# Two-layer hybrid trunk (attention, RWKV-7, DeltaNet, experts): passes, masks and odd projection reordered

## The chip, the cores and the metric

The kernel runs on one core of a Trainium2 chip. The metric is device microseconds for one execution. The kernel before takes 1800.96 us (median of 3 runs, 1800.35 to 1801.52). The engines are TensorE (PE), VectorE (DVE), ScalarE (ACT), GpSimd (POOL) and SyncE (SP, which issues the DMAs here).

## The reference, cut to what matters

Input x is 256 tokens of 1024 numbers, float32. Two layers follow each other.

- Even layer: h = rmsnorm(x); one projection gives q, k, v of 8 attention heads of 64 and r, k, v of 8 RWKV heads of 64. The attention output and the output of a bidirectional RWKV-7 scan are concatenated, projected and added to x. Then a dense SwiGLU of width 2816 is added.
- Odd layer: h = rmsnorm(x); one projection (1024 to 3600) gives, in chunks of 512 columns, c_b, c_c, c_x (a short gated convolution: y_c = c_b * conv3(c_c * c_x)), q, k, v of 4 DeltaNet heads of 128, a gate z, and 16 columns of beta and alpha. q, k, v go through conv3 and SiLU, q and k are scaled to unit length, and a chunked gated delta rule runs in both directions. Both parts are projected and added to x. Then the top 2 of 8 SwiGLU experts of width 3584 are added.

```
state = state * w + (state @ a) b^T + v k^T          # RWKV-7 step; y = state @ r
lhs = tril(kb k^T * decay, -1) + I                    # DeltaNet, per chunk
u = lhs^-1 (v * beta - (kb * exp(gc)) @ state)
o = (q * exp(gc)) @ state + (q k^T * decay) @ u
state = state * exp(glast) + (k * exp(glast - gc))^T u
```

Both scans are computed with chunks of 128 tokens. Every chunk of every head then needs the inverse of a unit triangular 128x128 matrix. There are 2 directions x 2 chunks x 8 heads of them for RWKV and 2 x 2 x 4 for DeltaNet.

## The kernel before, in words

The five engines run one program each, tied by semaphores. What an engine does next is the order in which its program is written; nothing is planned by a tool.

**Inverses.** The 16x16 blocks on the diagonals of all the matrices of a mixer are inverted together on DVE (`block_inverses`, L1312 to L1345: gather the blocks with a transpose, three doublings by products and sums, two transposes). Then three doubling levels (16 to 32, 32 to 64, 64 to 128; `lev` 4, 5, 6) run on PE, two groups `g` of four heads at a time. In a level POOL masks the matrix (`level_masks`, L630 to L642), PE multiplies it with the inverse so far (`X`, L2015), ACT copies X from PSUM, PE multiplies again (`PT`, L2027 and L2030), and DVE adds the result to P and T (`inv_adds`, L1360 to L1371). `expand` (L1347 to L1358) writes the block inverses as block-diagonal 128x128 tiles P and T.

**RWKV passes.** Four passes p = 0..3, one per (direction, chunk): (0,0), (1,1), (0,1), (1,0). Pass p needs, in order: the three levels of its inverse; the rest R (PE L2089, L2093) and its copy on ACT (L852); the update U = inverse x R (L2101) and its copy (L856); for p < 2 the states (L2110, L2112); the outputs (L2117, L2122, L2124), which DVE adds into `yab`. The score matrices are masked by DVE (`mask_scores`, L1373 to L1378), three masks m = 0, 1, 2 per pass: m = 0 is for the rest, 1 and 2 for the outputs. In the kernel before PE does all of a pass's levels, then waits for all six masks (two groups, three m) and then does rest, updates, states and outputs, group by group. After passes 0 and 1 it computes the scores of pass p + 2 (`score`, L2053, L2057), after pass 0 also `tokens(1)` (L2064), after pass 2 the transposes of the attention half (L2136). The attention output is scaled by 1/den (`attended`, L1303 to L1310) inside `block_inverses`, ahead of its second doubling. The output projection (`ev_half`, L2154) follows pass 3.

**Odd mixer.** PE: beta and alpha (L2242), then `od_in(0)` to `od_in(5)` (L2252; chunks in the order c_b, c_c, c_x, q, k, v; each is four column blocks of 128 in eight products of 256 columns, copied out by ACT, L917, from four PSUM banks in turn), with the sums of the gates after chunk 1 (L2268, L2270) and the squared lengths of q and k (`lengths`, L2260, a product with all ones into 128 partitions) between chunks; then z (L2282), k k^T and k q^T (L2290, L2291), transposes of k and v (L2298), the decay rows (L2306) and the beta rows (L2314). DVE does the short convolution (L1515 to L1525), then the convolutions of q, k, v as they come (`shift_mix`, L1140 to L1145), squares, reciprocals of 1024 columns (L1542), scales, then the decay differences (L1565, L1567), the matrices to invert `Ao` (L1577 to L1583), the gather (L1590), the block inverses, and the two inversion passes p = 4, 5 (`invert`), which PE starts at L2015 again. The recurrence, the gated norm, the output projection (L2359) and the router follow, and then 8 experts of about 124 us each, which load their weights in 336 DMAs of 1024 KB.

**Memory.** `arena`, `scr`, `ring`, `ehf` and `xn` are reused from stage to stage; `Tb` (the blocks to invert) lies in `Am`, the tile into which POOL writes its masked matrices; `attn` lies in the tile of hT, the input of all projections.

Of the kernel before, what the change touches and what calls it, by code (L numbers as in the profile page):

```python
# [8 lines left out]
ACT = mybir.ActivationFunctionType  # L9
# [33 lines left out]
NHOME = 4  # L43

# [10 lines left out]
    ("red_rdy qk_sum qk_rdy mix_rdy kinv_rdy mixv_rdy bon_rdy bon_cp ya_rdy blk_rdy ln1_sum y1_rdy ln0_sum yab_rdy "  # L55
     "sp_y g_rdy gc_rdy yc_rdy qk2_rdy blk2_rdy on_sum yd_rdy rt_max as_rdy").split())}
# [21 lines left out]
def static_chunks():  # L78
# [9 lines left out]
    if UPTO >= 3:  # L88
        out += [("od_in", n, 1) for n in range(7)] + [("od_out", n, 1) for n in range(2)]
# [3 lines left out]
def hybrid_trunk(nc, A, out):  # L93
# [19 lines left out]
    with ctx:  # L113
# [60 lines left out]
        class Region:  # L174
# [5 lines left out]
            def take(self, *shape):  # L180
# [4 lines left out]
                if len(shape) > 1:  # L185
# [79 lines left out]
        qkvr, qkvc, cbx = g_o.take(12, SEQ), g_o.take(12, SEQ), g_o.take(12, SEQ)  # L265
        cu, zt = g_o.take(4, SEQ), g_o.take(TT, 512)
        g_o2 = Region(arena, 0, 3072)
        Ao = g_o2.take(2, 8, P)
        Do = [g_o2.take(4, P) for _ in range(2)]
        Ug = Do  # L270
        attn = [[hT_f[:, 512 * (2 * i + g):512 * (2 * i + g) + 512].rearrange("p (u s) -> p u s", u=4)
                 for g in range(2)] for i in range(2)]
# [6 lines left out]
        kqm = [g_o4.take(4, P) for _ in range(TT)]  # L279
        Ro = [g_o4.take(4, P) for _ in range(2)]  # L280
# [6 lines left out]
        glog, nbeta = sm.take(TT, 8), sm.take(TT, 8)  # L287

# [30 lines left out]
        dve_const = sem("dve_const")  # L319
# [43 lines left out]
        ex_rdy = sem("ex_rdy")  # L363
# [35 lines left out]
        conv_rdy, silu_rdy, l2_sq, l2_ps, l2_std = (sem(n) for n in (  # L399
            "conv_rdy", "silu_rdy", "l2_sq", "l2_ps", "l2_std"))  # L400
# [32 lines left out]
        SC_BANK = [(0, 1, 2, 4), (4, 5, 6, 7)]  # L433
# [8 lines left out]
        def used_up(kind, n):  # L442
# [4 lines left out]
                    "od_in": (cv_ps, 2 * n + 2) if n < 6 else (z_ps, 2), "od_out": (o_ps, 8 + 2 * n + 2)}[kind]  # L447
# [130 lines left out]
        def _(pool):  # L578
# [19 lines left out]
            for a in range(TT):  # L598
# [10 lines left out]
                               pattern=[[-1, P]], channel_multiplier=1)  # L609
            link(pool.memset(bones[:, :], 0.0))  # L610
# [19 lines left out]
            def level_masks(p, mats, blocks):  # L630

                Am = INVB[p][3]
                for lev in range(LEV0, NLEV):
                    for g in range(2):
                        if lev > LEV0:
                            pool.wait_ge(x_ps, inv_seq(p, lev - 1, g))
                        elif p % 4 == 0:
# [6 lines left out]
            pool.wait_ge(dve_const, 1)  # L644
# [15 lines left out]
        def _(act):  # L660
# [167 lines left out]
            def score_copies(q):  # L828
                for i in range(8):
# [3 lines left out]
                    act.activation(scb[q % 2][i // 4][:, i % 4], B[SC_BANK[q // 2][i % 4]][:, 0:3 * P].rearrange(  # L833
# [67 lines left out]
            if UPTO >= 3:  # L901
# [3 lines left out]
                ba = B[6][:, 0:TT * 16].rearrange("p (a n) -> p a n", a=TT)  # L905
# [7 lines left out]
                def od_copies(m0, m1):  # L913
                    for m in range(m0, m1):
                        act.wait_ge(cv_ps, m + 1)
                        dst = cbx[:, 2 * m:2 * m + 2, :] if m < 6 else qkvr[:, 2 * m - 12:2 * m - 10, :]
                        act.activation(dst, B[m % 4][:, :].rearrange("p (t s) -> p t s", t=2),  # L917
                                       ACT.Copy).then_inc(cv_sb, 1)
# [6 lines left out]
                def od_length(i):  # L925
                    for n in range(2):
                        act.wait_ge(l2_ps, 2 * i + n + 1)
                        act.activation(xn[:, i, 512 * n:512 * n + 512], B[(6, 0)[i] + n][:, :], ACT.Sqrt,
                                       bias=eps_col[:, 0:1]).then_inc(l2_std, 1)

                od_copies(0, 5)
                act.wait_ge(dve_step, DVE_STEPS["gc_rdy"])
                act.activation(ge, gt, ACT.Exp).then_inc(act_step, 1)
                od_copies(5, 8)
                od_silu(0)
                od_copies(8, 10)
                od_length(0)
                od_silu(1)
                od_copies(10, 12)
# [128 lines left out]
        def _(dve):  # L1068
# [231 lines left out]
            for h in range(4, HA):  # L1300
                head_scores(h)
# [1237 lines left out]
```

## Time and profile before

| what | value |
|---|---|
| runs | 1800.35 to 1801.52 us, median 1800.96 |
| profiled execution | 1797.01 us, of which the span is 1795.3 us |
| mean granted TensorE clock | 0.963 of full |
| PE busy | 1704.0 us (95%) |
| DVE busy | 1306.4 us (73%) |
| ACT busy | 967.0 us (54%) |
| POOL busy | 78.9 us (4%) |
| DMA | 428.78 MB, mean 239 GB/s |

PE is busy almost everywhere. In the 40 slices of the span (44.9 us each) its busy tenths are below 7 in one place only, the fifteenth and sixteenth slice (628 to 718 us, digits 5 and 6). The granted clock is in tenths of full speed: 1.00 is 2.4 GHz and 0.50 is 1.2 GHz. The even mixer runs to 332 us, the dense SwiGLU to 527 us, the odd mixer and router to 788 us, and the experts to the end.

### The profile page before, as it was taken

What the parts mean: (1) busy time and instruction counts of PE and PEld (TensorE: products, weight loads), DVE (VectorE), ACT (ScalarE), POOL (GpSimd) and SP (SyncE); (2) the same over time, 40 slices, a digit from 0 to 9 for tenths busy, and PEclk for the clock granted to TensorE, in tenths of its full rate; (3) what the DMA queues carried; (4) which work ended last, traced back from release to release, by engine and by line L of the source; (5) the groups of instructions that cost most, each with busy time, mean ns of one, the idle gap of its engine ahead of it and who ended that gap; (6) DMA issues with size and microseconds to landing.
All of it is one profiled execution on the core that took longest, in us unless ns stands there. A gap on an engine that the chain in (4) does not pass through costs nothing.

```text
span 1795.3 us, 22588 instructions
## 1 busy us (share of the span) xinstructions
PE 1704.0 (95%) x8728; PEld 1414.3 (79%) x8728; DVE 1306.4 (73%) x1232; ACT 967.0 (54%) x905; POOL 78.9 (4%) x92
## 2 busy tenths in 40 slices
PE   7998999999999956989999999999999999999997
PEld 3867988699988835668888888888888888888886
DVE  5587555544430677468898888898888988888985
ACT  2455221444331231157767677777677677677773
POOL 1013321000000003000000000000000000000000
PEclk9998888999999988989999999999999999999999
DMA  6410002455542310089999999999999999999992
GB/s 230 136 59 0 1 1 94 140 184 185 190 169 94 141 47 1 7 287 372 369 334 367 376 330 362 352 353 366 336 363 375 322 369 375 326 368 353 346 372 100
DMA packets 199502, 428.78 MB, mean 239 GB/s; under 512 B 10746, under 2 KB 34574, under 8 KB 199438
## 3 DMA queue, kind: packets, MB, share of 16 engines
q1 hardware_dynamic: 199438, 427.90, 66.3%
q8 instruction: 44, 0.72, 0.2%
q14 instruction: 20, 0.16, 0.0%
HBM read 426.82 MB, written 1.05 MB: 238 GB/s over the span
## 4 chain that ended last, share of the span: by engine, by line
PE 91%; DVE 6%; ACT 1%; issue 1%; POOL 0%; DMA 0%; SPq 0%; DVEq 0%; ACTq 0%
PE bank L2416 17%; PE bank L2418 17%; PE bank L2417 17%; PE bank L2252 5%; PE bank L2185 4%; PE bank L2186 3%; PE bank L2184 3%; PE bank L2425 2%; PE bank L1842 2%; PE bank L2015 2%; PE bank L1833 2%; PE bank L2359 2%; PE bank L2154 2%; PE bank L2461 1%; PE bank L2030 1%; PE bank L2027 1%
## 5 line engine op out<-in xcount | busy, mean ns | idle before, releaser
L1778 DVE TENSOR_TENSOR split<-ring,split 128x2048 fp32r<-128x2048 f32 x336 | 763.8, 2289 | 113.3 <-ACT split L1051 109.7
L1051 ACT ACTIVATE split<-ring 128x2048 fp32r<-128x2048 f32 x336 | 640.2, 1924 | 175.5 <-PE bank L2418 173.9
L2416 PE MATMUL bank<-split 128*128 128x512 f32 x896 | 354.4, 395 | 2.7 <-DVE split L1752 1.4
L2418 PE MATMUL bank<-split 128*128 128x512 f32 x896 | 349.6, 390 | 0.0
L2417 PE MATMUL bank<-split 128*128 128x512 f32 x896 | 348.9, 389 | 0.0
L2416 PEld LDWEIGHTS bank<-split 128*128 128x128 f32 x896 | 168.3, 188 | 36.4 <-issue 1.7
L2418 PEld LDWEIGHTS bank<-split 128*128 128x128 f32 x896 | 168.2, 188 | 35.9
L2417 PEld LDWEIGHTS bank<-split 128*128 128x128 f32 x896 | 168.5, 188 | 33.5
L2416 PE MATMUL bank<-split,ehr_ 128*128 128x512 f32 x448 | 180.3, 402 | 0.0
L2418 PE MATMUL bank<-split,ehr_ 128*128 128x512 f32 x448 | 174.9, 391 | 0.0
L2417 PE MATMUL bank<-split,ehr_ 128*128 128x512 f32 x448 | 174.6, 390 | 0.0
L1469 DVE TENSOR_TENSOR ringr<-ring,split 128x2048 fp32r<-128x2048 f32 x33 | 75.5, 2293 | 90.0 <-ACT split L882 89.8
L2185 PE MATMUL bank<-ringr,split 128*128 128x256 f32 (+1 forms) x440 | 135.1, 307 | 0.0
L882 ACT ACTIVATE split<-ring 128x2048 fp32r<-128x2048 f32 x33 | 63.1, 1921 | 84.2 <-DMA ring<-in_ev_ffn_up 44.0
L2416 PEld LDWEIGHTS bank<-split,ehr_ 128*128 128x128 f32 x448 | 84.0, 188 | 28.1 <-DVE split L1778 10.5
L2184 PE MATMUL bank<-ehr_,split 128*128 128x256 f32 x352 | 99.1, 282 | 1.4 <-DVE ringr L1087 1.4
L2186 PE MATMUL bank<-ehr_,ringr 128*128 128x256 f32 x352 | 99.4, 282 | 0.0
L2418 PEld LDWEIGHTS bank<-split,ehr_ 128*128 128x128 f32 x448 | 84.1, 188 | 18.5
L2417 PEld LDWEIGHTS bank<-split,ehr_ 128*128 128x128 f32 x448 | 84.2, 188 | 15.9
L2185 PEld LDWEIGHTS bank<-ringr,split 128*128 128x128 f32 x440 | 83.6, 190 | 3.8
L2252 PE MATMUL bank<-scr,ring 128*128 128x256 f32 x384 | 85.5, 385 | 0.0
L2252 PEld LDWEIGHTS bank<-scr,ring 128*128 128x128 f32 x384 | 74.2, 194 | 10.8 <-issue 0.5
(461 smaller groups left out, 2153.3 us busy)
## 6 DMA issues: line engine op xcount, KB each, us to landing
ring<-in_od_moe_gate SPq DMA_DIRECT2D x112, 1024.0 KB, 7.0
ring<-in_od_moe_up SPq DMA_DIRECT2D x112, 1024.0 KB, 7.3
ring<-in_od_moe_down SPq DMA_DIRECT2D x112, 1024.0 KB, 6.6
ring<-in_od_w_in SPq DMA_DIRECT2D x7, 2048.0 KB, 7.8
ring<-in_ev_w_in SPq DMA_DIRECT2D x6, 2048.0 KB, 9.0
ring<-in_ev_ffn_gate SPq DMA_DIRECT2D x11, 1024.0 KB, 5.4
ring<-in_ev_ffn_up SPq DMA_DIRECT2D x11, 1024.0 KB, 7.9
ring<-in_ev_ffn_down SPq DMA_DIRECT2D x5, 2048.0 KB, 7.9
```

The lines of the kernel that those rows point to most:

```text
L882: act.activation(homes[q % NHOME], ring[:, v], ACT.Copy).then_inc(pc_hi, 1)
L1051: act.activation(wst[:, r % NSTAGE, 0, :], ring[:, (r % NHALF) * HALF:(r % NHALF + 1) * HALF], ACT.Copy).then_inc(w_hi, 1)
L1469: dve.tensor_tensor(ringr[:, v], ring[:, v], homes[q % NHOME].bitcast(F32), SUB).then_inc(pc_lo, 1)
L1778: dve.tensor_tensor(wst[:, r % NSTAGE, 1, :], ring[:, (r % NHALF) * HALF:(r % NHALF + 1) * HALF], wst[:, r % NSTAGE, 0, :].bitcast(F32), S ...
L1833: last = pe.matmul(B[banks[a]][:, :], hT[:, k, P * a:P * a + P], w8[:, k, :], start=(k == 0), stop=(k == KT - 1))
L2184: pe.matmul(o, sh, mh, start=start, stop=False, skip_group_check=True)
L2185: pe.matmul(o, sh, ml, start=False, stop=False, skip_group_check=True)
L2186: return pe.matmul(o, sl, mh, start=False, stop=stop, skip_group_check=True)
L2252: last = pe.matmul(B[m % 4][:, SEQ * (f % 2):SEQ * (f % 2) + SEQ], w8[:, k, P * f:P * f + P], hT[:, k, :], start=(k == 0), stop=(k == KT - 1))
L2416: pe.matmul(o, hi, wh, start=start, stop=False)
L2417: pe.matmul(o, hi, wl, start=False, stop=False)
L2418: return pe.matmul(o, lo, wh, start=False, stop=stop)
```

## The change

The maths is the same. In the RWKV part:

- PE's program for a pass is cut into pieces (`level_x`, `level_pt`, `rests`, `updates`, `outputs_v`, `outputs_u`, `states_v`, `states_u`) and put in another order. The rests stand inside level 6, between X and PT. The products with v stand before those with U. Each piece waits only for its own mask and group.
- DVE does one mask kind after each level. The tiles P and T of the next pass are expanded as soon as the one of them that the pass doesn't use, or no longer uses, is free. Two blocks of terms for the layer norm move from pass 2 into passes 0 and 1.
- `attended` moves behind the block inverses; it is one half per group. The clearing of `Tb` moves into the attention heads. `Tb` moves to `xn`, and POOL's first masks no longer wait for the block inverses.
- The scores of passes 1 and 3 use other banks or the same banks in another order, with other waits.

In the odd mixer:

- The projection order is q, k, c_c, c_x, c_b, v, z (`OD`), in pairs of column blocks and two banks. ACT writes the middle term of the convolutions while copying, and does the squares. The lengths of q and k are 8 rows instead of 128 equal ones: one reciprocal of 8x256, which PE then broadcasts.
- Decay rows, lengths, k k^T, k q^T, beta rows and the transposes of k stand between the projection chunks on PE. ACT gathers the blocks with 16 copies, so that DVE transposes them in one instruction. The block inverses and the short convolution stand ahead of v on DVE.
- `attn`, `Do`, `cbx`, `zt` move to other memory.

The diff, cut to its core ("..." marks what is left out):

```diff
+OD = (3, 4, 1, 2, 0, 5)
...
-        out += [("od_in", n, 1) for n in range(7)] + ...
+        out += [("od_in", n, 1) for n in OD + (6,)] + ...
...
+                        elif p == 0:
+                            pool.wait_ge(vt_sb, 2)
+                            pool.wait_ge(q_rdy, 4)
+                            pool.wait_ge(dve_step, DVE_STEPS["bon_cp"])
+                        elif p == 4:
                             pool.wait_ge(dve_step, DVE_STEPS[blocks])
...
+                def tile_copies(t):
+                    act.wait_ge(cv_ps, t + 1)
+                    n = OD[t // 2]
+                    src = B[t % 2][:, :].rearrange("p (t s) -> p t s", t=2)
+                    if n < 3:
+                        m = 4 * n + 2 * (t % 2)
+                        last = act.activation(cbx[:, m:m + 2, :], src, ACT.Copy)
+                    else:
+                        m = 4 * (n - 3) + 2 * (t % 2)
+                        act.activation(qkvr[:, m:m + 2, :], src, ACT.Copy)
+                        for i in range(2):
+                            b = cd + 12 + m + i
+                            last = act.activation(qkvc[:, m + i, :], src[:, i, :], ACT.Copy, scale=cols[:, b:b + 1])
+                    last.then_inc(cv_sb, 1)
...
+                for i in range(4):
+                    act.wait_ge(ao_rdy, i + 1)
+                    for k in range(4):
+                        r = slice(32 * k, 32 * k + 32)
+                        last = act.activation(strided(Qc2[r], 4 * i, (16, 2), (32, 32), (1, 4)),
+                                              strided(Ao[r], 512 * i + 32 * k, (0, 2), (1, 32), (P, 4)), ACT.Copy)
+                    last.then_inc(qc_rdy, 1)
+                tile_copies(7)
...
+            block_inverses(gather_all, None, whole(Xm), Tb, whole(Tm), Xs, Tc, Pc).then_inc(dve_step, 1)
+            dve.wait_ge(dve_step, DVE_STEPS["blk_rdy"])
+            for g in range(2):
+                expand_p(0, g, Pc)
+            for g in range(2):
+                expand_t(0, g, Tc)
+                attended(g)
+            for p, (z, c) in enumerate(RW):
+                inv_adds(p, 4)
+                mask_scores(p, 0)
+                inv_adds(p, 5)
+                mask_scores(p, 1)
+                inv_adds(p, 6)
+                mask_scores(p, 2)
...
+            for p, (z, c) in enumerate(RW):              # PE
+                for lev in range(LEV0, NLEV):
+                    for g in range(2):
...
+                        level_x(p, lev, g)
+                    if lev == NLEV - 1:
...
+                        for g in range(2):
+                            rests(p, g)
+                    for g in range(2):
+                        if lev == LEV0 and p == 0:
+                            if g == 0:
+                                pe.wait_ge(sc_sb, 15)
+                            else:
+                                pe.wait_ge(dve_step, DVE_STEPS["ya0_rdy"])
+                        level_pt(p, lev, g)
                 if p < 2:
+                    outputs_v(p, 0)
+                    outputs_v(p, 1)
+                    updates(p, 0)
+                    updates(p, 1)
                     pe.wait_ge(tok_sb, 2 * p + 2)
+                    states_v(p, 0)
+                    states_v(p, 1)
+                    states_u(p, 0)
+                    states_u(p, 1)
                 else:
+                    outputs_v(p, 0)
+                    updates(p, 0)
+                    updates(p, 1)
+                    outputs_v(p, 1)
+                outputs_u(p, 0)
+                outputs_u(p, 1)
...
+                od_pair(0)                                # PE, odd projection
+                od_pair(1)
...   (sums of the gates)
+                od_pair(2)
+                od_pair(3)
...   (decay rows)
+                od_pair(4)
+                for i in range(2):
+                    pe.wait_ge(l2_sq, i + 1)
+                    for h in range(HD):
+                        j = HD * i + h
+                        last = pe.matmul(B[2][0:HA, 0:SEQ], oneh[:, 7 - j:15 - j], xn[:, i, SEQ * h:SEQ * h + SEQ],
+                                         start=(j == 0), stop=(j == 2 * HD - 1))
+                last.then_inc(l2_ps, 1)
+                od_pair(5)
+                pe.wait_ge(dve_step, DVE_STEPS["linv_rdy"])
...   (8 products of 256 columns that broadcast the reciprocal lengths)
+                od_pair(6)
...   (k k^T, k q^T, beta rows)
+                od_pair(7)
+                pe.wait_ge(kk2_sb, 2)
+                for i in range(2):
+                    turn_tokens(i, 4)
+                for t in range(8, 12):
+                    od_pair(t)
+                pe.wait_ge(ao_rdy, 4)
...   (z; transposes of v; then the passes p = 4, 5)
```

## Rows read from the trace of the kernel before

**Rows 1.** RWKV stages: stretch, length, PE, PEld, DVE, ACT, POOL busy, clock, DMA.
```profile
174.10:192.65 18.55, 16.84 (x129) 16.43 (x129) 14.45 (x18) 3.16 (x6) 11.23 (x7) 0.87 0.00 1
192.65:210.59 17.94, 17.79 (x121) 16.99 (x121) 6.35 (x12) 5.01 (x12) 0.00 (x0) 0.74 0.01 1
210.59:243.78 33.19, 30.57 (x242) 29.58 (x240) 16.03 (x26) 8.39 (x19) 8.84 (x6) 0.90 0.01 1
243.78:279.40 35.62, 33.76 (x218) 33.26 (x217) 17.89 (x29) 6.27 (x14) 8.88 (x6) 0.73 0.01 2
279.40:303.71 24.31, 24.31 (x209) 24.08 (x209) 16.66 (x29) 5.91 (x12) 6.46 (x4) 0.98 0.24 86
```

**Rows 2.** TensorE's timeline, RWKV passes: start, duration, engine, line, count, [idle].
```profile
174.10 3.95 PE L2015 MATMUL bank<-arena 128*128 128x128 f32 x16 [4.83 <-POOL arena L642]
...
192.65 3.64 PE L2093 MATMUL bank<-scr,arena 128*128 128x64 f32 x16 [1.71 <-issue]
...
206.07 1.04 PE L2064 MATMUL bank<-ident,ring 128*128 128x128 f32 x8
207.05 0.70 PE L2053 MATMUL bank<-ring 64*128 64x256 f32 x4
...
210.59 2.05 PE L2015 MATMUL bank<-arena 128*128 128x128 f32 x16
...
216.12 2.17 PE L2015 MATMUL bank<-arena 128*128 128x128 f32 x16
...
227.40 1.97 PE L2093 MATMUL bank<-scr 128*128 128x64 f32 x16 [1.80 <-DVE scr L1378]
...
260.60 0.77 PE L2089 MATMUL bank<-scr,ring 128*128 128x128 f32 x2 [1.86 <-DVE arena L1378]
...
277.70 1.91 PE L2136 MATMUL bank<-ident,scr 128*128 128x128 f32 x8
```

**Rows 3.** VectorE's timeline, 159 to 211 us.
```profile
159.44 0.25 DVE L1305 RECIPROCAL small<-small 128x16 f32<-128x16 f32 x1 [1.04 <-PE bank L1936]
...
170.84 0.99 DVE L1345 STREAM_TRANSPOSE scr<-arena 128x512 f32<-128x512 f32 x1
171.87 6.73 DVE L1355 TENSOR_TENSOR arena<-scr,bmask 128x512 f32<-128x512 f32 x4
...
187.91 4.63 DVE L1378 TENSOR_TENSOR arena<-arena,smask 128x512 f32<-128x512 f32 x4
...
206.62 3.90 DVE L1355 TENSOR_TENSOR arena<-scr,bmask 128x512 f32<-128x512 f32 x4
```

**Rows 4.** Busy time by stage of the odd mixer.
```profile
539.56:655.30 115.74, 114.35 (x533) 93.88 (x532) 47.55 (x87) 32.54 (x47) 0.00 (x0) 0.98 0.31 109
655.30:685.68 30.38, 0.02 (x1) 0.03 (x1) 29.30 (x53) 3.61 (x7) 2.20 (x2) 0.57 0.00 0
685.68:737.80 52.12, 45.97 (x369) 44.33 (x370) 36.71 (x52) 10.42 (x17) 17.99 (x11) 0.96 0.01 1
```

**Rows 5.** TensorE's timeline of the odd mixer.
```profile
570.33 41.69 PE L2252 MATMUL bank<-scr,ring 128*128 128x256 f32 x192
611.85 1.88 PE L2260 MATMUL bank<-xn,ones 128*128 128x512 f32 x4
...
649.70 3.84 PE L2306 MATMUL bank<-tri,small 128*128 128x128 f32 x32 [1.39 <-ACT scr L952]
...
685.68 3.95 PE L2015 MATMUL bank<-arena 128*128 128x128 f32 x16 [30.36 <-POOL arena L642]
693.29 2.17 PE L2015 MATMUL bank<-arena 128*128 128x128 f32 x16
```

**Rows 6.** VectorE's timeline of the odd mixer.
```profile
665.50 5.69 DVE L1590 STREAM_TRANSPOSE arena<-arena 32x1024 f32<-32x1024 f32 x3
```

**Rows 7.** GpSimd's timeline at 132 us, copies of 32 partitions x 256.
```profile
132.37 4.18 POOL L649 COPY scr<-ring 32x256 f32<-32x256 f32 x4 [2.81 <-ACT ring L794]
```

**Rows 8.** ScalarE's timeline at 530 us, copies of 256 columns.
```profile
529.97 1.57 ACT L701 ACTIVATE scr<-bank,cols 128x256 f32<-128x256 f32 x4 [1.55 <-PE bank L1814]
```

More of the change, by code:

```diff
@@ L88, in static_chunks @@
     if UPTO >= 3:
-        out += [("od_in", n, 1) for n in range(7)] + [("od_out", n, 1) for n in range(2)]
+        out += [("od_in", n, 1) for n in OD + (6,)] + [("od_out", n, 1) for n in range(2)]
     return out
@@ L911, in _ @@
                 act.activation(gs, gs, ACT.Ln, bias=1.0).then_inc(act_step, 1)
[L913 to L918, printed above, removed]
+                cd, cc = COL["od_conv_dn"], COL["od_conv_c"]
+                def tile_copies(t):
[12 more added lines that the diff above has]
+                    last.then_inc(cv_sb, 1)
                 def od_silu(i):
@@ L1995, in _, with level_x @@
             values(HA - 1)
+            def level_x(p, lev, g):
+                Tm, Pm, Xm, Am = INVB[p]
+                n = inv_seq(p, lev, g)
+                if lev == LEV0:
+                    pe.wait_ge(ex_p, 2 * p + g + 1)
+                else:
+                    pe.wait_ge(tp_sb, n - 2)
+                pe.wait_ge(am_rdy, n)
+                pm = odd_even(Pm[g], lev, True)
+                for u in range(4):
+                    if lev == NLEV - 1 and INV[p][g][0] == 0:
+                        o, i = B[g][:, P * u:P * u + 64], pm[:, u, 0, :]
+                    else:
+                        o, i = B[g][:, P * u:P * u + P], Pm[g][:, u, :]
+                    last = pe.matmul(o, Am[g][:, u, :], i, start=True, stop=True)
+                last.then_inc(x_ps, 1)
@@ new lines, in level_pt @@
+            def level_pt(p, lev, g):
+                Tm, Pm, Xm, Am = INVB[p]
+                end, z = lev == NLEV - 1, INV[p][g][0]
+                if lev == LEV0:
+                    pe.wait_ge(ex_t, 2 * p + g + 1)
+                pe.wait_ge(x_cp, inv_seq(p, lev, g))
+                xm = odd_even(Xm[g], lev, True)
+                tm = odd_even(Tm[g], lev, False)
+                for u in range(4):
+                    if not (end and z == 1):
+                        last = pe.matmul(packed(B[2 + g], lev, 0)[:, u], Tm[g][:, u, :], xm[:, u],
+                                         start=True, stop=True)
+                    if not (end and z == 0):
+                        last = pe.matmul(packed(B[2 + g], lev, 64)[:, u], Xm[g][:, u, :], tm[:, u],
+                                         start=True, stop=True)
+                last.then_inc(pt_ps, 1)
@@ new lines, in outputs_u, with states_v @@
+            def outputs_u(p, g):
+                pe.wait_ge(u_sb, 2 * p + g + 1)
+                pe.wait_ge(msk_rdy, 6 * p + 4 + g + 1)
+                for u in range(4):
+                    last = pe.matmul(B[4 + g][:, DH * u:DH * u + DH], scb[p % 2][g][:, u, 2, :], Um[g][:, u, :],
+                                     start=False, stop=True, skip_group_check=True)
+                last.then_inc(y_ps, 1)
+            def states_v(p, g):
+                c = RW[p][1]
+                for q in range(2):
+                    j = 2 * g + q
+                    pe.matmul(B[g][:, P * q:P * q + P], tokbk[:, 1, j, :], vtok[:, c, P * j:P * j + P],
+                              start=(q == 0), stop=False, skip_group_check=True)
```

569 lines of the change are left out of this document (292 added, 277 removed).

## The prediction

> **What bounds the kernel now.** I read the page's busy tenths first: TensorE (PE) is full except in two places, the RWKV passes (126 to 304 us) and the odd mixer. So the question is where PE waits and at which clock it runs. The busy time by stretch answers both. In the RWKV passes PE is busy 123.3 of the 129.6 us from 174.1 to 303.7, but its granted clock is 0.87, 0.74, 0.90 and 0.73 in the first four stretches and 0.98 in the last one, which has no idle time [rows 1]. TensorE's timeline shows what comes ahead of each fall: an idle gap of 4.83 us (waiting for POOL's first mask), then 1.71, 1.80 and 1.86 us ahead of the rests of passes 0, 1 and 2 [rows 2]. In the odd mixer PE is busy 114.4 of 115.7 us up to 655.3, then idle for 30.4 us while VectorE (DVE) is busy 29.3 of them, and the clock is 0.57 meanwhile [rows 4, 5]. During the 115.7 us before, DVE was busy 47.6 us only [rows 4]. So one part is bound by waits and clock, the other by a DVE chain that starts when the projections are over. The experts follow on PE, at its full load, and the change doesn't touch them.
>
> **RWKV, the start.** Block inverses before end with the transpose at 170.84 + 0.99 = 171.8 [rows 3]. They held a wait of 1.04, a reciprocal and two scalings (`attended`, 159.44 to 160.94, so 1.04 + 1.5 = 2.5 us; the second doubling starts at 160.94), and about 1.0 us of clearing. Both leave: 171.8 - 3.5 = 168.3. The clearing goes between two attention heads, where DVE waits for PE; if that cover were gone it would cost its 1.0 us again. POOL's first masks are made before, so X(0) waits for one P tile per group: 3.90 / 4 = 0.97 us each when POOL is quiet [rows 3]. X starts at 169.4 instead of 174.1: 4.7 us. Behind it T tiles and the two scalings alternate on DVE while POOL makes its level 5 masks; beside POOL an expansion takes 6.73 / 4 = 1.68 us [rows 3]. Expansion of T(0) to 171.9, scaling 172.8, T(1) 174.4, scaling 175.1, add 175.8 and 176.4: level 4 takes until 176.2, 1.3 us more than 5.5. PE idles twice for about 0.6 us there.
> The Trainium skill (SBUF — State Buffer, Who interferes with whom) says that a two-input DVE operation and a GpSimd read exclude each other for a whole instruction. By that rule two scalings or expansions could each stand behind a whole POOL mask, some 1.5 us more in all; the rows show 0.71 us per expansion. I take the rows.
>
> **RWKV, the passes.** Work of a pass at full clock, from the only stretch that runs so: pass 3 takes 24.3 us [rows 1]. Pass 2 adds the attention transposes, 1.9 [rows 2]: 26.2. Pass 1 has no products with states (8 of 128 columns less), 8 such products for new states (as many more, so no change), and the scores, 207.05 to 210.59 = 3.5 [rows 2]: 27.8. Pass 0 adds `tokens(1)`, 1.0 us, the time from the end of the outputs to 207.05: 28.8. Sum 107.1, plus 1.3 for the start = 108.4; passes end at 169.4 + 108.4 = 277.8 instead of 303.7: 25.9 us. In parts: 4.7 of start - 1.3, about 5.9 of gaps (1.71 + 1.80 + 1.86 and half a microsecond ahead of scores), and 16.6 of clock. The last is the biggest term and isn't bought by any instruction; it follows only if the gaps are what makes the clock fall.
> Does the new order have no gap? Mask 0 (two masks, 4.63 / 4 = 1.16 us each beside POOL [rows 3]) has the whole of level 5 until the rests need it. PE's level is 216.12 - 210.59 = 5.53 us [rows 2], DVE's share of it 1.5 for the adds and 2.3 for masks: fits. Mask 2 is due 5 us after the last product of level 6, with 1.9 of updates, 1.8 of products with v and more in between. ACT's copies of R hide behind level 6's second half, those of U behind the state products. Expansions for the next pass (3.90 for four [rows 3]) lie beside outputs and scores. Moved layer-norm terms (8 operations of 0.7 us) lie behind pass 0 and 1, where DVE has 8 us until the next add. Where an ACT copy of scores is late, 0.3 us stay; I count no more.
> Bounds of the clock term: if it doesn't return at all, 0; if all the shortfall returns, 0.13 x 18.6 + 0.26 x 17.9 + 0.10 x 33.2 + 0.27 x 35.6 = 20.0 us [rows 1], of which a part is gap time anyway. 16.6 is between them and nearer to the upper end, because pass 3, the same kinds of product with no gap, ran at 0.98.
>
> **Odd mixer, what PE does until the inversion.** Removed: the idle 30.4 us [rows 5] and the 1.4 us before the decay rows [rows 5]. Added: lengths are 8 products of 256 columns, and 8 more broadcast the reciprocals; a product of 256 columns is two records of 41.69 / 192 = 0.217 us [rows 5], so 16 x 0.43 = 6.9 us, less two old ones of 1.8: +3.4. All other products are the same, in another order. So PE reaches the first X at 685.7 - 31.8 + 3.4 = 657.3 (less the RWKV gain), if nothing stalls it. Its first level then runs at full clock: 693.29 - 685.68 = 7.6 becomes 5.5 [rows 2, 5]: 2.1. Sum 30.4 us.
> What covers what: on that clock the decay rows end at 574, so differences and exponentials are done at 583, and both unit-length scales at 596; k k^T is due at 602 and 603.5, `Ao` is ready at 610. ACT gathers with 16 copies of 256 elements: 16 x 1.57 / 4 = 6.3 us taken [rows 8]; POOL's copy of the same shape took 1.05 [rows 7], so up to 16.7 us as the other bound (no less than 0.2 each). Pair 7 ends at 614, and DVE waits for its copy ahead of the c_c * c_x product. From there DVE has at most what it did in the idle stretch before, 29.3 us [rows 4], and the short convolution's eight shifted sums of half a microsecond each, 4.2: ready at 648, where PE comes at 657. Without the differences and `Ao`, which are done by then (12 us), and with one transpose of 1.2 us for four (5.69 for three [rows 6]), it is about 632. Some 25 us of cover; with the slow bound of the copies still 15. v's convolution ends at 647, its SiLU at 648; due at 656. The tightest are the pairs' two banks: a pair is 6.9 us, its three copies 1.5 us, so a stall needs ACT held for 5 us ahead of a copy. ACT is held so by its waits for the differences (until 583, pair 6 is due at 595) and for `Ao` (until 612; pair 9 is due at 622). With the slow copies pair 9 stalls 1.5 us. I take no stall.
> From the second level on the order is as before: same gaps of 1.1 to 1.7 us, clock 0.96 over 52 us [rows 4]. Chunk loads keep their order and slots; nothing on SP's queue moves but by the same shift.
>
> **Sum.** 25.9 + 30.4 = 56.3 us. The profiled execution took 1797.0 (span 1795.3), so 1740.7; the runs' median is 1800.96, 4.0 above it, so I predict 1744.7 for the median.
>
> **Rivals.**
> (1) The clock doesn't return in the passes. For: in the stretch 243.8 to 279.4 it stayed low long after a gap of 1.86 us, so these products of 64 columns may not lift it; and two gaps of 0.6 us stay at the start. Against: 0.98 in pass 3, and 1.1 to 1.7 us gaps in the odd inversions with 0.96 [rows 1, 4]. Time: 16.6 lost, 1761.
> (2) A stall in the projections or late blocks, with DVE or ACT stopped at a wait that was put ahead of other work. The place is an ACT or DVE wait that comes more than 5 us later than I count; one such overshoot of 10 us costs PE 5 to 10: 1750 to 1755. Against: each cover above is 5 us or more.
> (3) The whole gain of the odd mixer fails, because the inversion waits for z and v, which now stand last, and DVE's passes wait with it: then only the RWKV gain stays, 1775. Against: no step of the chain to the blocks needs z or v.
> (4) Slower: the matmuls set between the chunks (8 rows of output, copies waited for) make the clock fall in the projections, which ran at 0.98 [rows 4]. At 1.2 GHz a stretch takes twice its time, so it decides from 56 us of the 118 us on: all of it would be +62 net, 1807. Against: the longest filler takes 3.8 us [rows 5] and products of 256 columns stand around them, as in the kernel before.
>
> **How the numbers follow.** Forecast 0.58, own range 1739 to 1749. Rival (1) in whole or part 0.20; (2) 0.13; (3) 0.05; (4) 0.02; 0.02 is left for no change. A change below 0.2% (3.6 us) can't be told from none here. Faster 0.96, same 0.02, slower 0.02. The range of 8 in 10 reaches from the clock term's upper bound (20.0 instead of 16.6, 1741, and 1.5 us less) to rival (1): 1739 to 1765.
>
> **What would show it.** Right: no PE wait above 1 us from 170 to 278 us, granted clock above 0.95 in it, four passes of 24 to 29 us; in the odd mixer the projections and their fillers in one piece of 118 us, X of p = 4 directly behind the transposes of v, and DVE's last block transpose about 50 us earlier in the span and long before PE comes. Wrong: a clock of 0.5 in passes without gaps (the largest term falls), or an idle PE in front of a pair or of X. Experts should take what they took.

## The result and the profile after

The changed kernel took 1746.6 us in the median of four runs (1740.05 to 1750.98) and the kernel before, on the same chip beside it, 1801.2 us: ratio 0.970, 95% interval 0.967 to 0.973, so 54.6 us faster. Run again later the medians were 1743.7 and 1807.0 (ratio 0.966, 0.961 to 0.970). The forecast was 1744.7 us. The profiled execution after took 1750.98 us; its span of 1749.3 us is 46.0 us less than the span of the one before.

Where these 46.0 us are, by the starts of the same work in both traces (the forecast's parts are rounded):

| stretch | before | after | difference | forecast |
|---|---|---|---|---|
| start to X of pass 0 | 174.10 | 184.79 | +10.7 | -4.7 |
| the four RWKV passes | 129.61 | 103.79 | -25.8 | -21.2 |
| to the odd mixer's transposes | 224.66 | 223.10 | -1.6 | 0 |
| odd mixer to X of p = 4 | 157.31 | 130.26 | -27.0 | -28.4 |
| the rest | 1109.6 | 1107.4 | -2.3 | -2.1 |
| sum | | | -46.0 | -56.3 |

The page after, parts 1 and 2: PE is up from 95% to 97% of the span although it works 6 us less.
```profile
span 1749.3 us, 22670 instructions
...
PE 1697.8 (97%) x8752; PEld 1403.4 (80%) x8752; DVE 1274.8 (73%) x1212; ACT 980.8 (56%) x934; POOL 76.9 (4%) x94
...
PE   7999999999999998899999999999999999999997
...
PEclk9995999999999999899999999999999999999999
```
The hole of the fifteenth and sixteenth slice is gone. The 5 in the fourth place of the clock row (131 to 175 us) is what the forecast did not have: the attention heads.

The four passes after, one row each (stretch, length, PE, PEld, DVE, ACT, POOL busy, clock, DMA); the same work as [rows 1]:
```profile
184.79:213.03 28.24, 28.09 (x251) 27.06 (x249) 19.68 (x34) 9.14 (x21) 9.28 (x6) 1.00 0.01 1
213.03:240.35 27.32, 27.02 (x243) 26.20 (x241) 17.12 (x30) 8.40 (x19) 8.83 (x6) 1.00 0.01 1
240.35:264.96 24.61, 24.61 (x219) 24.38 (x218) 15.77 (x25) 5.91 (x14) 9.11 (x6) 1.00 0.01 1
264.96:288.58 23.62, 23.62 (x210) 23.39 (x209) 11.81 (x22) 6.27 (x13) 5.67 (x4) 1.00 0.26 90
```
PE's idle time is 0.45 us in all (before: 6.3), and the clock is 1.00 in each (before 0.73 to 0.90 in the first four rows). In PE's timeline of the heads, ahead of the passes:
```profile
131.54 1.12 PE L2055 MATMUL bank<-ident,scr 128*128 128x128 f32 x4 [2.65 <-ACT scr L813]
...
142.67 1.12 PE L2055 MATMUL bank<-ident,scr 128*128 128x128 f32 x4 [2.23 <-ACT scr L813]
143.58 3.42 PE L2072 MATMUL bank<-head_ind,ehf 128*128 128x8 f32 x16
```
and PE's busy time and clock in the stretches around them:
```profile
124.00:142.67 18.67, 13.68 (x88) 0.88 0.32 114
142.67:179.00 36.33, 34.96 (x156) 0.50 0.00 0
```
For 36 us PE is all but fully busy and runs at 1.2 GHz. TensorE's program for the heads is the one of before, where the mean clock from 124 us to X was 0.80.

The odd mixer after, PE's timeline; it answers to [rows 5]:
```profile
515.43 5.44 PE L2390 MATMUL bank<-wsmall,scr 128*128 128x16 f32 x32 [1.58 <-ACT scr L712]
520.71 15.65 PE L2401 MATMUL bank<-scr,ring 128*128 128x256 f32 x64
...
561.93 3.62 PE L2435 MATMUL bank<-xn,small 128*8 128x256 f32 x16
565.48 7.17 PE L2401 MATMUL bank<-scr,ring 128*128 128x256 f32 x32
572.58 4.71 PE L2445 MATMUL bank<-kinv,ident 8*128 8x256 f32 x16
577.22 9.51 PE L2401 MATMUL bank<-scr,ring 128*128 128x256 f32 x32
...
627.34 13.90 PE L2478 MATMUL bank<-ring,scr 128*128 128x512 f32 x32
641.07 1.04 PE L2407 MATMUL bank<-ident,arena 128*128 128x128 f32 x8
641.94 1.95 PE L2097 MATMUL bank<-arena 128*128 128x128 f32 x16
```
X of p = 4 (last row) follows the transposes of v with nothing between: 30.36 us of idle time are gone, and its first level takes 647.37 - 641.94 = 5.4 us, not 7.6. DVE and ACT meanwhile:
```profile
621.28 1.02 DVE L1392 STREAM_TRANSPOSE xn<-arena 128x512 f32<-128x512 f32 x1
622.34 5.82 DVE L1396 TENSOR_TENSOR arena<-xn,bmask 128x512 f32<-128x512 f32 x4
```
```profile
590.83 10.57 ACT L988 ACTIVATE ehf<-arena 32x256 f32<-32x256 f32 x16
...
633.55 1.06 ACT L944 ACTIVATE arena<-arena 128x1024 f32<-128x1024 f32 x1 [3.38 <-DVE small L1597]
```
The block inverses are ready at 622.3, the SiLU of v ends at 634.6, and PE wants it at 641.07: 6.5 us of slack for v, some 13 for the blocks.

### The profile page after: what moved, and what is told of

The parts are those of the page before. It is cut to its first block, busy times and chain, and to the rows that moved or that the text cites. A ratio compares the mean times of both kernels' runs of the same rounds, so it can differ in the third digit from the quotient of the medians.

```text
span 1749.3 us, 22670 instructions
## 1 busy us (share of the span) xinstructions
PE 1697.8 (97%) x8752; PEld 1403.4 (80%) x8752; DVE 1274.8 (73%) x1212; ACT 980.8 (56%) x934; POOL 76.9 (4%) x94
## 4 chain that ended last, share of the span: by engine, by line
PE 94%; DVE 3%; ACT 1%; issue 1%; DMA 0%; SPq 0%; DVEq 0%; ACTq 0%
PE bank L2585 18%; PE bank L2587 17%; PE bank L2586 17%; PE bank L2401 5%; PE bank L2333 4%; PE bank L2334 4%; PE bank L2332 4%; PE bank L1927 2%; PE bank L2594 2%; PE bank L2097 2%; PE bank L1918 2%; PE bank L2528 2%; PE bank L2302 2%; PE bank L2114 1%; PE bank L2111 1%; PE bank L2630 1%
## 5 line engine op out<-in xcount | busy, mean ns | idle before, releaser
L2585 PEld LDWEIGHTS bank<-split,ehr_ 128*128 128x128 f32 x448 | 84.0, 188 | 28.3 <-DVE split L1863 10.6
L2586 PEld LDWEIGHTS bank<-split,ehr_ 128*128 128x128 f32 x448 | 84.2, 188 | 15.9
```

The costliest lines, as they stand in the source:

```text
L2585: pe.matmul(o, hi, wh, start=start, stop=False)
L2586: pe.matmul(o, hi, wl, start=False, stop=False)
```

## The experiments

Kernels of one group ran on the same chip and share the runs of the kernel before. Its median was 1804.1 in the first group, 1807.0 in the second, 1801.1 in the third and 1800.2 in the last.

**Each half alone (first group).** The old text of the other half is kept, with its order and waits.
```
odd_only:   RWKV functions, POOL's first masks, score banks   as before
rwkv_only:  OD, od_pair, tile_copies, ACT's and DVE's odd order  as before
```


> Only the odd mixer is changed; the RWKV part keeps the old order (block inverses with the attention scaling in them, rests behind all masks). My theory: the odd mixer's idle time of 30.4 us is gone here too, and the first level of the inversion is warm, so -30 us against the kernel before (about 1771 us), and the RWKV passes show their old gaps of 1.7 to 1.9 us and their old clock of 0.73 to 0.90. Rival (the two parts help each other through the clock): less than -22 us.

Measured: 1776.8 us, -27.3 (ratio 0.983, 0.977 to 0.988). Its passes took 134.1 us at a mean clock of 0.81, with gaps of 1.70, 1.80 and 1.86 us, as before. X of p = 4 (678.90) follows the transposes of v (678.03) with no wait. The measured gain is near the expected 30 us, and the interval (21 to 41 us) holds both it and, barely, the rival's 22.

> Only the RWKV part is changed; the odd mixer keeps its old order and its idle 30 us. My theory: start, gaps and clock together give -10 to -26 us (1775 to 1791), the low end where the attention heads run at 0.5, as they did in the changed kernel's profile, and the high end where they don't; the passes take 104 to 109 us at a granted clock above 0.95 either way. Rival (the passes' clock comes from something else than their gaps): passes at 0.75 to 0.9 and only -9 us.

Measured: 1771.6 us, -32.5 (ratio 0.979, 0.973 to 0.985): 6.5 us more gain than the largest that was expected, a miss in size. The passes took 103.9 us at 1.00, and PE still waits 30.5 us for POOL in the odd mixer. In its trace the heads had a better clock (0.82 from 124 us on), and X came at 179.89. By the medians the halves add up (27.3 + 32.5 = 59.8 against 54.6 and 63.4 for both in two groups). So nothing speaks for the rival that they need each other, though each half is known to some 10 us only.

**What the start is worth, at equal clocks.** In odd_only's trace the attention heads happened to get the same low clock as in the changed kernel's, and the last scores start within 0.1 us of each other. Only the work ahead of X differs. odd_only, with the old start, then the changed kernel:
```profile
183.12 0.70 PE L2112 MATMUL bank<-ring 64*128 64x256 f32 x4 [0.30 <-ACT scr L840]
...
190.33 3.96 PE L2065 MATMUL bank<-arena 128*128 128x128 f32 x16 [5.52 <-POOL arena L649]
```
```profile
183.17 0.70 PE L2146 MATMUL bank<-ring 64*128 64x256 f32 x4 [0.30 <-ACT scr L844]
...
184.79 2.05 PE L2097 MATMUL bank<-arena 128*128 128x128 f32 x16
```
X comes 5.5 us earlier with the new start. The traces in which the heads ran faster (rwkv_only, gap_back, rows128, heads_fill2, best) keep a wait of 1.5 to 1.9 us ahead of X: there the scores end before VectorE's first expanded tile is ready. The profile names an ACT copy as what ended this wait, but in heads_fill2 that copy ended at 170.8, while the block inverses end at 170.6, the first tile comes about 1 us later, and X starts at 171.76. With fast heads the wait thus falls from 4.83 to about 1.9 us and not to zero.

**Is it the gaps that take the clock? (first group).** The largest term of the forecast, 16.6 us, stood on this. One kernel fills the gaps of the kernel before without removing them:
```
                 pe.wait_ge(sc_sb, 8 * min(p + 2, 4))
+                if p < 3:
+                    pe.wait_ge(tok_sb, 2 * min(p + 1, 2))
+                    for _ in range(8):
+                        pe.matmul(B[6][:, 0:P], ident[:, :], ident[:, :], start=True, stop=True)
                 pe.wait_ge(msk_rdy, 6 * p + 6)
```


> The kernel before, and nothing moved: only in passes 0 to 2, while TensorE waits for the masks ahead of the rests, it multiplies the identity by itself 8 times (8 x 0.22 us at full clock, into a bank that is free). The wait for the masks is as long as before, only not idle. My theory (the idle gaps make the clock fall): the granted clock of the passes rises from 0.73..0.90 to above 0.95 and most of the clock term comes back without a gap removed: -10 to -17 us (1784 to 1791). Rival (the narrow products of the passes, or the busy share, make it fall, and the new order brought it back otherwise): 0 to +2 us, clock as before.

Measured: 1788.2 us, -15.9 (ratio 0.989, 0.984 to 0.994). Its passes, by PE's busy time and clock:
```profile
188.23:217.00 28.77, 28.77 (x240) 0.94 0.01 1
217.00:249.60 32.60, 31.64 (x285) 1.00 0.01 2
249.60:300.75 51.15, 50.56 (x442) 1.00 0.12 42
```
They sum to 112.5 us where the kernel before has 129.6, and the masks are waited for as before. The 17.1 us are clock alone. The other kernel puts a gap back into the changed one:
```
                 if p < 3:
                     mask_scores(p, 2)      # ahead of inv_adds(p, 6)
-                pe.wait_ge(msk_rdy, 6 * p + g + 1)
+                pe.wait_ge(msk_rdy, 6 * p + (6 if p < 3 else g + 1))
```


> The changed kernel, but in passes 0 to 2 VectorE makes the third mask ahead of the last adds, and the rests wait for it, as in the kernel before: a gap of about 2 us per pass is back, nothing else. My theory: the clock falls again behind these gaps, so +6 us for the gaps and 10 to 16 us for the clock: 1760 to 1770 us. Rival (the gaps cost only themselves): +6 us, about 1753, passes at a clock above 0.95.

Measured: 1781.9 us (ratio 0.988, 0.982 to 0.993), 35 to 38 us above the changed kernel's two medians (in other groups): a miss in size, on the side of the theory. Passes of this kernel, the gaps in stretches of their own:
```profile
187.00:190.59 3.59, 0.06 (x2) 0.94 0.00 0
190.59:227.00 36.41, 36.26 (x248) 0.77 0.00 1
227.00:230.47 3.47, 0.00 (x0) 1.00 0.00 0
230.47:266.10 35.63, 35.33 (x240) 0.76 0.00 1
266.10:269.64 3.54, 0.01 (x2) 0.86 0.00 0
269.64:315.82 46.18, 46.18 (x313) 0.75 0.14 46
```
Passes: 142.1 us, 38.3 more than the changed kernel's 103.8. The gaps are 3.5 us each and not 2, since two mask kinds (4.63 us) now stand behind the adds of level 5, ahead of the rests: 10.6 us. The other 27.7 us are clock. After the last gap PE has 46 us without any idle time, and the mean clock is 0.75: it is 0.50 to 292.5 us and 1.00 from then on. One idle gap of 3.5 us is followed by 23 us at half speed, some 11 us lost.

**The heads (second to fourth group).** Five runs ask why the clock is 0.5 there and what it costs.

> The changed kernel as it is, run again beside the three others so that they have it to be compared with, and for the spread of its time. Two executions of it in two traces are to show whether the clock of 0.5 in the attention heads is always there. My theory: the heads' code is the same as before, and whether the clock falls behind head 0 or head 2 (gaps of 2.65 and 2.23 us) differs from run to run: 1740 to 1751 us, with X of the first pass between 169 and 186 us. Rival (the change itself slowed the heads): X at 184 to 186 us in each trace.

Measured: 1743.7 us (1734.5 to 1751.3), X at 184.79 once more. X at 184.8 in both traces is what the rival had named. Yet it isn't the change that slows the heads: of the three traces with the old RWKV part, two (odd_only and fill_gaps) have a clock of 0.68 there, as low as the changed kernel's 0.66, and only the one of before has 0.80, and two kernels with the new RWKV part (rwkv_only, gap_back) have X at 179.89 and 173.77. The ten times of the changed kernel go with their mean granted clock: 0.987 and 0.985 at 1734.7 and 1734.5 us, 0.977 at 1751.

```
+                for _ in range((10, 0, 8, 0, 0, 0, 3, 3)[h]):
+                    pe.matmul(B[2 + 2 * (h % 2)][:, 0:P], ident[:, :], ident[:, :], start=True, stop=True)
                 pe.wait_ge(att_e, h + 1)
```


> The changed kernel, with TensorE multiplying the identity by itself where it waits for the first exponentials of a head: 10 products at head 0, 8 at head 2, 3 each at heads 6 and 7. My theory: no idle gap above 1 us stays from 112 us on, so the granted clock stays above 0.95 through the heads and the passes, X of the first pass comes at about 170 us instead of 184.8, and the time is 1735 to 1741 us with a smaller spread. Rival (narrow products of 64 and 8 columns make the heads' clock fall): clock 0.5 to 0.8 in the heads as before, time unchanged.

Measured: 1745.0 us (1736.6 to 1749.0), X at 180.93: no gain, 4 us above the range. The gaps it aimed at were down to 0.2 and 0.3 us, but one of 1.77 us appeared at head 1 (135.03 us). The clock stayed at 1.00 behind it for 9 us and fell to 0.50 at 144 us, behind the bonus products (behind head 2, products of 8 columns each that sum RWKV's bonus term by head). Two suspects, told apart by three more kernels: bonus products interleaved with identity products (bonus_fill), that and the waits of heads 0, 1, 2 filled (heads_fill2), and the waits filled alone (gaps_only).
```
+                            pe.matmul(B[7][:, 0:P], ident[:, :], ident[:, :], start=True, stop=True)
                             last = pe.matmul(B[6][:, HA * a:HA * a + HA], bonT[...], head_ind[:, j, :], ...)
```


> The changed kernel, with one product of the identity by itself (128 columns) ahead of each of the 8 products of 8 columns that make the bonus behind head 2; nothing else. What it asks: with the gaps at heads 0 and 2 filled, the clock still fell to 0.5 at 144 us, right behind these narrow products. Theory A (products with 8 columns make it fall, as the 16-column ones do at the start of the odd mixer): the clock in the heads stays above 0.9 behind them in this kernel, unless a gap has brought it down before. Theory B (the gaps of 2.65 and 2.2 us bring it down): 0.5 in the heads from 142 us on as in the changed kernel's trace, time 1740 to 1747 us.

Measured: 1746.3 us. The clock is 0.50 from 142 to 178 us; the gaps of 3.12 and 1.80 us had brought it down, so this run says nothing on the bonus products.

> The changed kernel, with identity products in the waits of heads 0, 1 and 2 (10, 8 and 8 of them) and ahead of each bonus product. My theory: gaps and narrow products are both covered, so the granted clock stays above 0.9 from 112 us to the end of the passes, X of the first pass comes at 170 to 174 us, and the time is 1733 to 1738 us. Rival (a clock of 0.5 there has another cause, such as the products of 64 columns with 64 rows): as with the changed kernel, 1744 us.

Measured: 1741.4 us (1737.3 to 1744.3), 3 us above the range, X at 171.76. The clock is 1.00 from 112 to 160 us and falls for 4 us behind three waits of 0.5 to 0.7 us at heads 6 and 7. The gain by the medians is 2 to 5 us and not the 13 us of the earlier X. Of these 13 us, 3.3 lie ahead of head 0, where the edit does nothing; and the profiled run is one of the fast ones. Probably part of the runs of the changed kernel have a good clock in the heads without help, but no trace of such a run is kept.

> The changed kernel, with identity products in the waits of heads 0, 1 and 2 (10, 8 and 8), and the bonus products left as they are. With both covered the clock stayed at 1.00 to 160 us; with heads 0 and 2 covered alone it fell at 144 us, behind the bonus products, but there was an idle gap of 1.77 us ahead of head 1 too. Theory A (the narrow bonus products make it fall): 0.5 behind them again, X of the first pass at 180 us or later. Theory B (the gap at head 1 did): 1.00 through the bonus products, X at 170 to 172 us, and the time of the kernel with both covered, 1741 us, or 1 to 2 us less.

Measured: 1738.5 us (1733.0 to 1745.0), X at 175.15, between what the two theories named. No idle time from 131.7 to 152 us, and yet (PE's timeline, then its clock by stretches):
```profile
142.44 0.66 PE L2057 MATMUL bank<-ident,scr 128*128 128x128 f32 x4
142.94 1.85 PE L2074 MATMUL bank<-head_ind,ehf 128*128 128x8 f32 x16
144.72 1.13 PE L2013 MATMUL bank<-scr 64*128 64x256 f32 x4
145.77 1.57 PE L2021 MATMUL bank<-scr 128*128 128x64 f32 x8
147.13 1.06 PE L2057 MATMUL bank<-ident,scr 128*128 128x128 f32 x4
```
```profile
144.00:146.00 2.00, 2.00 (x14) 1.00 0.00 0
146.00:148.00 2.00, 2.00 (x12) 0.56 0.03 8
```
The same transposes take 0.66 us ahead of the bonus products and 1.06 us behind them. So the clock can fall behind products of 8 columns without a gap, but it doesn't each time. In the trace of the kernel before the same 16 records ran at full clock, and it stayed at 1.00 until 156 us (its timeline, then stretches behind them):
```profile
139.71 1.85 PE L1987 MATMUL bank<-head_ind,ehf 128*128 128x8 f32 x16
141.49 1.13 PE L1928 MATMUL bank<-scr 64*128 64x256 f32 x4
```
```profile
142.00:145.00 3.00, 3.00 (x31) 1.00 0.00 0
145.00:148.00 3.00, 2.68 (x21) 1.00 0.00 0
148.00:151.00 3.00, 3.00 (x29) 1.00 0.02 5
```
Of three traces that came to the plain bonus products at full clock, two (heads_fill, gaps_only) lost it behind them; the two with identity products between (heads_fill2, best) did not. What it costs varies too: the fall lasted 3 us in gaps_only and 27 us in heads_fill. From head 0's transposes to X, gaps_only takes 43.4 us (131.74 to 175.15) and heads_fill2 43.5 (128.22 to 171.76), so in these two traces the identity products between the narrow ones cost what they gave back; the earlier X of heads_fill2 comes from ahead of the heads. By the medians the variants with filled heads (1738.5, 1741.4) can't be told from each other, and hardly from the changed kernel (1743.7 and 1746.6).

**Products over 8 rows (second group).** In the odd mixer the clock fell to 0.5 behind L2445.
```
-        kinv = sb("kinv", [HA, SEQ])
+        kinv8 = sb("kinv", [P, SEQ])        # zero from row 8 on
-    ident[0:HA, j:j + 1].to_broadcast([HA, P]), kinv[:, :]
+    ident[:, j:j + 1].to_broadcast([P, P]), kinv8[:, :]
```


> The changed kernel, with the 8 reciprocal rows of the unit lengths widened to 128 rows (rows 8 to 127 zero), so that the 8 products that broadcast them in the odd mixer contract over 128 rows and not over 8; columns, order and waits are the same. My theory: the clock falls to 0.5 behind the 8-row products in the changed kernel (they take 4.7 us where the 128-column rate would give 3.5, and the pair behind them 9.5 us, where a warm one takes 7.0); with all rows it stays above 0.95, and the stretch is 3 to 4 us shorter. Rival (the fall has another cause there): the pair behind takes 9 us as before.

Measured: 1745.0 us (1736.6 to 1747.1), the same as the changed kernel within the spread; the trace decides.
```profile
571.54 3.62 PE L2447 MATMUL bank<-kinv,ident 128*128 128x256 f32 x16
574.99 7.07 PE L2403 MATMUL bank<-scr,ring 128*128 128x256 f32 x32
```
4.71 + 9.51 became 3.62 + 7.07: 3.5 us. This doesn't rest on one draw: all nine traces with these products over 8 rows have 4.3 to 4.7 us and 9.5 to 9.9 us for the two rows, and the two traces with 128 rows (this and best) have 3.62 and 7.07. The added rows hold zeros only, so it isn't the data that counts.

The even mixer has products over 8 rows as well (8 records in 1.99 us, at 84.44 us in the changed kernel), in the same code in every kernel. Within 3 us behind them the clock fell to 0.50, for 6 to 11 us, in 10 of the 14 traces; in the other four (before, gap_back, heads_fill2, best) it stayed at 1.00.

**The cover of the odd mixer (second group).**
```
+                for _ in range(2):
+                    link(dve.reciprocal(osum[...], cu[...]))   # 128 x 1024
                 unit_blocks(whole(Am2))
```


> The changed kernel, with two more VectorE operations of 1024 columns ahead of the odd mixer's block inverses (reciprocals into a buffer that is overwritten later): at the 1741 ns of a reciprocal of 256 columns some 13.9 us. My theory: VectorE's chain to the first X has 19 us of slack for the blocks, so they are ready in time; v's convolution and SiLU have 6.5 us, so the transposes of v wait about 7 us and the time is 6 to 8 us above the changed kernel's. Rival (the cover is more than I read, or VectorE's chain still sets the start): 0, or 13 us.

Measured: 1751.0 us (ratio 0.971, 0.966 to 0.976), 7.3 above the changed kernel of its group, inside the expected 6 to 8. PE's wait and what follows it, in its timeline:
```profile
647.60 1.97 PE L2410 MATMUL bank<-ident,arena 128*128 128x128 f32 x8 [6.68 <-ACT arena L944]
649.36 2.98 PE L2100 MATMUL bank<-arena 128*128 128x128 f32 x13
```
The wait is 6.7 us, on the SiLU of v and on nothing else, as expected; the blocks, ready 13 us later too (635.3), cost nothing. Behind it the transposes take 1.97 us, not 1.04: the way from them to the second level's X takes 2.8 us more than in the changed kernel.

**All together (third group).** heads_fill2, rows128, and the 16 products of 16 columns (L2390) one by one between the 16 dense ones of the first pair.
```
                 last = pe.matmul(B[t % 2][...], w8[:, k, c:c + P], hT[:, k, :], ...)
+                if t == 0:
+                    nb = pe.matmul(B[2][:, 16 * f:16 * f + 16], hT[:, k, P * f:P * f + P], ba_w[:, k, :], ...)
```


> The kernel of the run with all head waits and bonus products filled, and two more edits: the reciprocal rows of the unit lengths over 128 rows (shown to keep the clock, 3.5 us), and the 16 products of 16 columns at the start of the odd mixer set one by one between the dense products of the first pair. My theory: the three places where the clock falls outside of long waits are gone, so 3.5 us for the rows and 3 to 4 us for the narrow products come on top: 1726 to 1732 us. Rival (the clock falls at the next gap instead, 1.6 to 1.8 us ahead of the odd mixer): 3.5 us at most.

Measured: 1734.7 us (1731.7 to 1745.6; ratio 0.966, 0.963 to 0.968), 2.7 above the expected range, 6.7 below heads_fill2 of its group, and 9 to 12 below the changed kernel's two medians, in another group. Six runs and ten runs with a deviation of 6 us each differ by 6.5 +- 3 us in their means, so faster than the changed kernel is likely, not proven. From 503 to 522 us, through the interleaved products, the clock is 1.00 (0.50 to 0.56 from 517 to 524 in the changed kernel), and X of p = 4 comes 123.25 us behind the odd mixer's first transpose (499.11 to 622.36) instead of 130.26: 7.0 us, which is what was expected of the two odd-mixer edits. Four of the six runs took 1731.7 to 1734.8 us; the other two, at 1745 us, have a mean clock of 0.982 (0.989 to 0.992 in the four), so something still costs clock in part of the runs.

## Why the prediction was right, and where it was not

The forecast for the median was 1.9 us off, but that closeness is partly luck. In the profiles the gain was missed by 10.3 us (46.0 instead of 56.3): the profiled execution before was faster than the median beside it (1797.0 against 1801.2), the one after slower (1751.0 against 1746.6). And terms of 15 us and of 5 us were off in opposite directions. What was right is the mechanism of the two large terms, the gaps with their clock and the idle time of the odd mixer.

- **What bounds it: right.** The two stretches named, passes and odd mixer, gave 52.8 us in the profile.
- **The start, -4.7 us: the edit did it, the total did not show it (+10.7).** The idle 4.83 us ahead of X [rows 2] are gone, POOL's first mask is made 20 us ahead (164.14), and X follows the last scores with nothing between. At equal clocks (odd_only) the edit is worth 5.5 us. But I took the time up to there from the one trace of before as fixed. It isn't: X comes 15.4 us later than forecast, 3.9 of them by the start of v's projection (113.03 against 109.09 us), behind the even mixer's products over 8 rows, and the rest in the heads. The trace of before was a good draw in both places. Three of the ten runs of the changed kernel (1734.5 to 1740.1 us, mean clock 0.984 to 0.987) meet or pass the profile's forecast of 1740.7; that they lack these falls is likely, but none of them was traced.
- **The rule of the Trainium skill** (SBUF — State Buffer, Who interferes with whom) would have added some 1.5 us at the first level. The expansion and the second scaling beside POOL's masks at 186.03 took 1.04 and 0.68 us against 0.99 and 0.69 without them, so VectorE paid nothing, and leaving the 1.5 us out of the sum was right. This doesn't refute the rule. POOL's two masks took 2.89 us there (3.60 in heads_fill2) against 2.49 alone at 164.14, so POOL may have been the one that waited, where it delayed nothing. And the rule is for two inputs in SBUF; the scalings read one of theirs from PSUM, so my reading applied it to them wrongly.
- **Gaps, 5.9 us: right.** 0.45 us of idle time are left of 6.3. What the sum did not have is the wait of 1.5 to 1.9 us ahead of the first X in the traces with fast heads.
- **Clock, 16.6 us: right in kind, 19.9 in the profiles** (PE's busy time in the passes fell from 123.28 to 103.34 us at the same work). The cause is shown by filling the gaps (17.1 us back, no wait removed) and by putting them back (27.7 us lost beside the 10.6 of the gaps). Rival 1, that the narrow products keep the clock down, falls: they run at 1.00 for 104 us. It holds in one sense only: once down, the clock stayed down for 23 us of such products without idle time (gap_back).
- **Pass lengths, 108.4 us: 4.6 too long.** This is the same error as the clock term's (3.3 us) plus the 1.3. Measured were 28.2, 27.3, 24.6 and 23.6 us, forecast 28.8 (+1.3), 27.8, 26.2 and 24.3. The 1.3 for a slow first level didn't come (5.53 us from X to X), and the 1.9 for the attention transposes in pass 2 was read from a row at half clock [rows 2]; here they take 1.04.
- **Odd mixer, 30.4 us in all: 29.3 measured.** Idle 30.4 gone and the first level 2.2 shorter, as forecast. Lengths and broadcasts: 3.62 + 4.71 instead of 6.9, and 2.4 for the pair behind, which ran at half clock. This is rival 4 in the small; its price was 3.5 us, not 62, since the fall lasted 7 us and not to the end of the projections. The clock was low at the narrow products of beta and alpha both before (0.50 from 530 to 543 us, from the wait ahead of them on) and after (517 to 523.5 us).
- **Cover: right by a narrower margin than told.** ACT's gather took 10.57 us (0.66 each) against 6.3 taken and 16.7 bounded. v's SiLU was ready 6.5 us ahead (8 forecast), and the run with 13 us more work on DVE turned that into a wait of 6.7. Rivals 2 and 3 fall.

## What to carry over

On an engine whose clock falls when it idles, price a wait with what follows it: here gaps of 1.8 us cost about 6 us each in slow products (17.1 for three), gaps of 3.5 us about 9 (27.7 for three), although a single gap of 1.77 us was once followed by 9 us at full clock (heads_fill). When a gap can't be removed, products into a free bank inside the wait give most of that back (15.9 us for 24 idle products). And a stretch at a lower clock in one trace is a draw, not a constant: look at a second execution before you use its length, and compare two kernels where both had the same clock, as odd_only and the changed kernel had up to X.

## Hardware behaviour not expected

- Products that contract over 8 rows with 256 columns (16 records, odd mixer) were followed by a granted clock of 0.50 with no idle time around them in nine of nine traces; over 128 rows, 120 of them zero, in none of two. A group of 8 such records in the even mixer was followed by it in 10 of 14.
- Products of 8 columns (128x8, 16 records in 1.85 us) were followed by a fall to 0.50 with no idle time around them in two of three traces.
- How long a fall lasts isn't told by the shape of the products behind it. With the heads' products of 64 to 256 columns behind the fall, the clock was back after 3 us (gaps_only, 146 to 149.5), after 7 (rwkv_only, 134 to 141) or after 36 (the changed kernel, 142 to 178.5). With dense products of 256 columns behind the 8-row products of the odd mixer it was back in 7 us.
- The same code is granted different clocks in the same place: over these traces 0.63 to 1.00 from 88 to 100 us and, with no wait filled, 0.66 to 0.82 in the heads. The times of the changed kernel spread by 17 us and its mean clock from 0.977 to 0.987; a stretch at 0.50 loses half its length, so 0.010 of mean clock over 1744 us is some 17 us lost (an estimate), and the clock can account for most of the spread.
